# Rotary partners by transfers, square sums reordered ahead of one long sum, gated tiles split two steps later, in a two-block fp32 layer kernel

## The reference

```
x1, x2 = xr[..., :half], xr[..., half:]
rot = concatenate([x1 * c - x2 * s, x2 * c + x1 * s], axis=-1)
```

## Time and profile before

| what | value |
|---|---|
| median of 3 runs | 1926.7 us (1924.33 to 1930.63) |
| profiled execution, its time | 1925.77 us |
| profiled execution, its span | 1924.5 us |
| PE busy | 1909.5 us, 99% of the span |
| DVE, ACT, POOL busy | 1174.6, 880.2, 312.5 us |
| mean granted clock of PE | 0.996 |

### The profile page before, as it was taken

One profiled execution on the slowest core, in us unless ns is written; L12 is line 12 of the kernel. 1 busy time (PEld: TensorE's weight loads), 2 busy tenths in 40 slices (PEclk: granted clock), 3 DMA queues, 4 the chain that ended last, 5 costly groups with the idle time before them and its releaser, 6 DMA issues.

```text
span 1924.5 us, 37152 instructions
## 1 busy us (share of the span) xinstructions
PE 1909.5 (99%) x15818; PEld 1875.1 (97%) x15818; DVE 1174.6 (61%) x1709; ACT 880.2 (46%) x1265; POOL 312.5 (16%) x317
## 2 busy tenths in 40 slices
PE   9999999999999999999999999999999999999999
PEld 8999999999999999999999999999999999999987
DVE  6765666655555556645654765675467786555744
ACT  6444454544444434444444533445443333444443
POOL 3210010202110003300211252040011132110300
PEclk9999999999999999999999999999999999999999
DMA  7565545556666555565565563544564444566564
GB/s 259 155 198 180 162 155 156 176 186 188 196 189 195 196 192 183 185 202 195 191 237 196 167 217 121 154 132 130 156 183 146 133 143 138 181 199 195 194 232 154
DMA packets 175921, 343.80 MB, mean 179 GB/s; under 512 B 10495, under 2 KB 19579, under 8 KB 175227
## 3 DMA queue, kind: packets, MB, share of 16 engines
q1 hardware_dynamic: 174106, 337.16, 55.1%
q10 hardware_dynamic: 1648, 4.26, 0.6%
HBM read 335.09 MB, written 6.29 MB: 177 GB/s over the span
## 4 chain that ended last, share of the span: by engine, by line
PE 89%; issue 3%; DVE 2%; POOL 2%; ACT 0%; POOLq 0%; DVEq 0%; ACTq 0%
PE bank L1303 88%; DVE w_lo L1946 1%; POOL arena L2534 1%; DVE ob L2182 0%; POOL scratch L2540 0%; POOL arena L2543 0%; DVE hb L2182 0%; ACT w_hi L1638 0%; DVE scratch L2052 0%; POOL scratch L2551 0%; PE bank L1520 0%; PE bank L1610 0%; PE bank L1460 0%; PE bank L1458 0%; PE bank L1459 0%
## 5 line engine op out<-in xcount | busy, mean ns | idle before, releaser
L1946 DVE TENSOR_TENSOR w_lo<-w_raw,w_hi 128x1024 fp32r<-128x1024 f32 (+2 forms) x644 | 788.1, 1228 | 467.5 <-ACT w_hi L1638 465.4
L1638 ACT ACTIVATE w_hi<-w_raw 128x1024 fp32r<-128x1024 f32 (+2 forms) x644 | 662.4, 1032 | 874.2 <-PE bank L1303 863.9
L1303 PE MATMUL bank<-hb,w_hi 128*128 128x256 f32 x5284 | 957.1, 279 | 3.8 <-DVE w_lo L1946 2.1
L1303 PEld LDWEIGHTS bank<-hb,w_hi 128*128 128x128 f32 x5284 | 814.8, 188 | 7.4 <-DVE w_lo L1946 5.1
L1303 PE MATMUL bank<-ob,w_hi 128*128 128x256 f32 (+1 forms) x4060 | 773.4, 284 | 0.8 <-DVE w_lo L1946 0.8
L1303 PE MATMUL bank<-hb,w_lo 128*128 128x256 f32 x2448 | 678.1, 277 | 0.0
L1303 PEld LDWEIGHTS bank<-ob,w_hi 128*128 128x128 f32 x4060 | 635.4, 188 | 4.5 <-DVE w_lo L1946 1.2
L1303 PE MATMUL bank<-ob,w_lo 128*128 128x256 f32 (+1 forms) x2224 | 622.5, 280 | 0.0
L1303 PEld LDWEIGHTS bank<-hb,w_lo 128*128 128x128 f32 x2448 | 461.2, 188 | 0.0
L1303 PEld LDWEIGHTS bank<-ob,w_lo 128*128 128x128 f32 x2224 | 418.6, 188 | 0.0
L1303 PE MATMUL bank<-w_hi,ob 128*128 128x512 f32 (+1 forms) x384 | 104.2, 358 | 0.0
(11 more groups left out here) (239 smaller groups left out, 1039.9 us busy)
## 6 DMA issues: line engine op xcount, KB each, us to landing
w_raw<-in_w_in SPq DMA_DIRECT2D x436, 512.0 KB, 3.6
w_raw<-in_w_out SPq DMA_DIRECT2D x64, 512.0 KB, 4.3
w_raw<-in_w_o_conv SPq DMA_DIRECT2D x32, 512.0 KB, 4.1
w_raw<-in_w_o_mla SPq DMA_DIRECT2D x32, 512.0 KB, 4.0
w_raw<-in_w_branch SPq DMA_DIRECT2D x32, 512.0 KB, 3.7
w_raw<-in_w_kv_b SPq DMA_DIRECT2D x16, 512.0 KB, 3.9
w_raw<-in_w_q_b SPq DMA_DIRECT2D x16, 384.0 KB, 3.2
arena<-x_kept SPq DMA_DIRECT2D x2, 2048.0 KB, 9.8
```

Of the source, the lines that this page charges most:

```text
L1303: return nc.tensor.matmul(dst, lhsT, rhs, start=start, stop=stop, skip_group_check=True)
L1638: act(dst, src, ACT.Copy).then_inc(S_("w_hi"), 1)
L1946: tt(low, src, high.bitcast(F32), ALU.subtract).then_inc(S_("w_lo"), 1)
```

## The change

1. `rope` for the 28 tiles of `qr`, `qi`, `ka` and `qa` no longer uses PE. A new step `rope_swap` lets SP copy rows of x into the scratch buffer with partners exchanged (4 transfers for `qr` and `qi`, 2 for `ka` and `qa`; 128 rows of 1 KB in all), two pumps ahead of the step `rope`. The sign moves into the sine tables. DVE multiplies the scratch buffer by the sine table in place; POOL waits for the transfers before it writes x. The shared keys keep the products on PE (`rope_key`). A `qr` or `qi` job is two pumps longer, a `ka` or `qa` job one.
2. `row_sum` multiplies all but the last of the separate squares ahead of the accumulator.
3. After `row_sum` of `rp` come two of the constant products, then `row_spread`, then one (before: `row_spread`, then five).
4. The splits in `zconv`, `zmla`, `omla` and `bb` come 9 tiles after the evacuation, in `za` and `zb` still 7.

```diff
@@ _constants @@
-    put("rot_q1", rotation(RD, RD // 2, 1))
-    put("rot_a", rotation(P, 16, 1))
-    put("rot_i1", rotation(DI, 8, 1))
+        sign = np.where(o < half, -1.0, 1.0)[:, None]
+        return np.where(on, np.cos(ang), 1.0), np.where(on, sign * np.sin(ang), 0.0)
@@ plan_work @@
-    def rope(kind, k, ready, tables, rows=P):
-        dup = kind in ("kr", "ki")
-        b, s, b2 = side.take(), scratch.take(), None
...
+    def rope(kind, k, ready, tables):
+
+        sc = scratch.take()
+        landed = f"ld_rot{sc.slot}"
+        t = add("rope_swap", kind, k, dma=f"{landed} " * len(SWAPS[kind]), scratch=sc, ready=ready)
+        yield
+        yield
+        st = add("rope", kind, k, marks="rope_sin rope_out", scratch=sc, ready=ready, landed=t[landed], tables=tables)
+        sc.ends(st["rope_out"])
         done[kind, k] = st["rope_out"]
...
             def split_y():
                 done["oc", k] = add("conv_split", j, m, marks="op_hi op_lo", y=s["gated"])["op_lo"]
                 conv_free[m] = [("oc", k)]
-            later(split_y, 7)
+            later(split_y, 9)
...
-            later(split_y, 7)
+            later(split_y, 9 if name == "zm" else 7)
...
     post = row_factor("rp", [done["out_sq"]], extra=out_extra)
+    next(post)
+    warm(2)
     post_bank, done["rp"] = yield_of(post)
-    warm(5)
+    warm(1)
...
-        yield
-        yield
-        rope("ka", k, s["normed"], "late")
+        yield
+        yield from rope("ka", k, s["normed"], "late")
...
-        yield
-        rope("qa", h, s["qa_scaled"], "late")
+        yield from rope("qa", h, s["qa_scaled"], "late")
@@ new table @@
+SWAPS = {"qr": [(at + to, at + 32 - to, 32) for at in (0, 64) for to in (0, 32)],
+         "qi": [(at + to, at + of, n) for at in (0, 64) for to, of, n in ((0, 8, 8), (8, 0, 56))],
+         "qa": [(0, 16, 16), (16, 0, 112)]}
+SWAPS["ka"] = SWAPS["qa"]
@@ sync_engine @@
+    def rope_swap(s):
+        x, use = m.rope_of(*s.args)[0], s.of["scratch"]
+        sp.wait_ge(*use.after)
+        sp.wait_ge(*s.of["ready"])
+        for to, of, n in SWAPS[s.args[0]]:
+            dma(m.scratch[use.slot][to:to + n, 0:x.shape[1]], x[of:of + n, :]).then_inc(S_(f"ld_rot{use.slot}"), 16)
@@ tensor_engine, row_sum @@
+        early, late = s.of["extra"][:-1], s.of["extra"][-1:]
+        for i, (use, mark) in enumerate(early):
+            pe.wait_ge(*mark)
+            for j, lo in enumerate(starts):
+                mm(b[0:w, j:j + 1], m.scratch[use.slot][0:rows, lo:lo + w], ones[0:rows, 0:1], i == 0 and j == 0, False)
         for mark in s.of["squares"]:
             pe.wait_ge(*mark)
@@ vector_engine @@
     def rope(s):
+        x, _, cos, sin, _, _ = m.rope_of(*s.args)
+        partner = m.scratch[s.of["scratch"].slot][:, 0:x.shape[1]]
+        ve.wait_ge(*s.of["landed"])
+        ve.wait_ge(*done[s.of["tables"]])
+        tt(partner, partner, sin, ALU.mult).then_inc(S_("rope_sin"), 1)
@@ pool_engine, rope @@
+        po.wait_ge(*s.of["ready"])
+        po.wait_ge(*s.of["landed"])
```

More of the change, by code:

```diff
@@ L64, in rotation @@
             if o < half:
-                r[base + o + half, m] = -1.0
+                r[base + o + half, m] = 1.0
             elif o < 2 * half:
@@ L387, in factor, with rope_key @@
         done[what] = s["rf_out"]
-    def rope(kind, k, ready, tables, rows=P):
-        dup = kind in ("kr", "ki")
-        b, s, b2 = side.take(), scratch.take(), None
-        st = add("rope", kind, k, marks="rope_rot rope_sin rope_out" + (" rope_dup rope_cos" if dup else ""),
-                 bank=b, scratch=s, ready=ready, tables=tables, dup=Use(side, 0, NEVER))
+    def rope_key(kind, ready, tables):
+        b, s, b2 = side.take(), scratch.take(), side.take()
+        st = add("rope_key", kind, 0, marks="rope_rot rope_sin rope_out rope_dup rope_cos",
+                 bank=b, scratch=s, ready=ready, tables=tables, dup=b2)
         b.ends(st["rope_sin"])
+        b2.ends(st["rope_cos"])
         s.ends(st["rope_out"])
-        if dup:
-            b2 = st.of["dup"] = side.take()
-            b2.ends(st["rope_cos"])
+        done[kind, 0] = st["rope_out"]
+    def rope(kind, k, ready, tables):
[6 more added lines that the diff above has]
+        sc.ends(st["rope_out"])
         done[kind, k] = st["rope_out"]
@@ L402, in rope_later @@
         yield
-        rope(kind, k, ready, tables)
+        if kind == "kr":
+            rope_key(kind, ready, tables)
+        else:
+            yield from rope(kind, k, ready, tables)
         for _ in range(rest):
@@ L788, in ki_job @@
         yield
[L789 removed]
+        rope_key("ki", s["ki_gain"], "late")
         pending.extend(index_head(h) for h in range(HI))
@@ L1382, in row_sum @@
         for j, lo in enumerate(starts):
-            inst = mm(b[0:w, j:j + 1], squares[0:rows, lo:lo + w], ones[0:rows, 0:1], j == 0, not s.of["extra"])
-        for use, mark in s.of["extra"]:
+            inst = mm(b[0:w, j:j + 1], squares[0:rows, lo:lo + w], ones[0:rows, 0:1], j == 0 and not early, not late)
+        for use, mark in late:
             pe.wait_ge(*mark)
@@ L1434, in rope @@
         mm(m.side[b.slot][:, 0:w], rot[0:rows, :], x[0:rows, :]).then_inc(S_("rope_rot"), 1)
[L1435 to L1438, removed]
+        b = s.of["dup"]
+        pe.wait_ge(*b.after)
+        mm(m.side[b.slot][:, 0:w], dup[0:rows, :], x[0:rows, :]).then_inc(S_("rope_dup"), 1)
     def scores1(s):
@@ L2508, in rope @@
     def rope(s):
-        x, rot, cos, sin, dup, rows = m.rope_of(*s.args)
-        if dup is None:
-            po.wait_ge(*s.of["ready"])
-            po.wait_ge(*s["rope_rot"])
-            po.wait_ge(*done[s.of["tables"]])
-            t = po.step(tt(x, x, cos, ALU.mult))
-            po.wait_ge(*t)
-            po.wait_ge(*s["rope_sin"])
-            tt(x, x, m.scratch[s.of["scratch"].slot][:, 0:x.shape[1]], ALU.add).then_inc(S_("rope_out"), 1)
+        x, _, cos, _, _, _ = m.rope_of(*s.args)
+        po.wait_ge(*s.of["ready"])
+        po.wait_ge(*s.of["landed"])
+        po.wait_ge(*done[s.of["tables"]])
+        t = po.step(tt(x, x, cos, ALU.mult))
+        po.wait_ge(*t)
+        po.wait_ge(*s["rope_sin"])
+        tt(x, x, m.scratch[s.of["scratch"].slot][:, 0:x.shape[1]], ALU.add).then_inc(S_("rope_out"), 1)
     def clear_meta(s):
```

37 lines of the change are left out of this document (18 added, 19 removed).

## The result

The changed kernel takes 1909.5 us in the median of four runs (1907.83 to 1910.57), the kernel before 1925.5 us on the same chip (four runs, 1924.09 to 1930.63). The ratio is 0.992, 95% interval 0.9905 to 0.9934. The profiled execution took 1908.9 us. The forecast was 1910.0 us.

A forecast was written before the change was run, and what follows sets the result against it. PE was taken as the bound. Terms -12.2 + 0.5 - 0.5 - 3.5 - 1.0 = -16.7 us took the profiled 1925.8 to 1909.1, or 1910 us against the median of 1926.7; range 1905 to 1918.

The forecast's parts named there:

- Rotary products, -12.2 us: `q`, `qi`, `ka`, `qa`: 28 products leave PE, 24 at 0.43 us and 4 at 0.46, all of it gained.
- Waits for landings, +0.5 us: Rotary stages: DVE now waits for swap transfers to land; +0.5 us in all, bounds 0 and 7.
- a tie at 4.1 us: `q`: a swap lands 0.4 + 1.9 + 1.8 = 4.1 us on, DVE comes to it after some 4.2 us.
- rival C: `q`: DVE waits 1 to 2 us per landing, costing 7.6 us, so 1917 to 1918 us (1920 with later stages); chance 0.10.
- a sign of being wrong: `q` or `ka`: the prediction is wrong if PE waits for `w_lo` there; no size given.
- Rival D: Swaps in `q` and `qi`: four transfers land one after another, 7.2 us after issue; +31 us, so 1941; chance 0.06.
- Later splits, -3.5 us: `zconv` and `zmla`: five PE waits for `w_lo` go, 0.69 us each; bounds 3.5 and 0.
- End of wout, -1.0 us: End of `wout`: `qi` starts up to 2.3 us sooner, less a clock cost; -1.0, between -2.5 and +1.5.
- `qi` at the lower clock: Start of `qi`: after PE idles about 1 us, up to 5 us at half pace cost 2.5 us.
- Attention's jobs, -0.5 us: Moved job queue: a 1.6 us eviction stall goes, a new meeting can cost as much; -0.5, between -1.6 and +2.

The follow-up runs named there:

- no_swap: The kernel before with the later splits and the reordered end of `wout`, rotary products still on PE; 1920.4 us, ratio 0.9976.
- eight_issues: The changed kernel with each swap transfer cut in two by columns, 176 issues for the same bytes; 1944.5 us.
- split7: The changed kernel with every split of a gated or merged tile back at 7 tiles; 1914.7 us, 1914.1 without one run of 2081 us.
- early_q: The changed kernel with DVE's and POOL's rotary steps of `q` one pump later behind their swap, three instead of two; 1907.4 us.
- both: The changed kernel with every second swap transfer issued by ACT and the rotary steps of `q` one pump later; 1908.0 us, ratio 0.9897.
- pool_queue: The changed kernel with all 88 swap transfers issued by POOL instead of SP; 1931.8 us.

## Why the prediction was right

**Rotary products, -12.2 us: right.** In the aligned starts a swap's unit is 0.24 + 0.19 = 0.43 us shorter in `q` and in `qi`, as read from the earlier trace rows. The median of no_swap, which keeps these products, is 10.9 us higher; that is net of the waits for landings and holds some clock and pace (above). DVE's product itself took 0.42 us from SBUF as it had from PSUM.

**Waits for landings, +0.5 us: the term that was mis-sized.** It measured about 5 us: `q` gained 1.1 us where eight products are 3.44, and 1085 to 1172 us gained 0.7 where eight more are 3.44, so 2.3 + 2.7. The issue was taken as 0.47 us from the earlier trace rows, and it was 0.60 in `q` and 0.75 behind `qi`. For `q` I had written that the landing is a tie at 4.1 us after the first issue; it came to 4.25 (89.42 to DVE's start at 93.67) and 5.9 (93.56 to 99.42). In the second the issues took 2.4 us (1.9 forecast) and the time behind the last of them 3.45 (1.8 forecast), so in `q` the larger miss is behind the issues; what holds those transfers is open. For `qi` I had counted DVE's room and not SP's, which was full. So rival C happened in small: its place was right, and its price in `q` was 2.3 us and not 7.6, since DVE waited at six of the eight swaps and PE felt it at three places. One of the three is a wait of PE for `w_lo`, 0.5 us at 101.9 us. The prediction had named that as a sign of being wrong, and for this term it was.

**Rival D's mechanism** didn't occur at its size. The last of four transfers landed 1.4 us after its issue ended (1128.10 + 3.01 = 1131.11, DVE at 1132.53), and not after four landings of 1.8 us in a row. The Trainium skill's rule on disjoint parts ("DMA: Bandwidth & Descriptors", section "Rules for kernel authors") did not show as added time of that size, and the 1941 us of rival D did not come; with issues 0.6 to 0.75 us apart, a shorter transfer could still wait for its neighbour unseen. The other half of that rule, one transfer in place of several, is borne out, through the issues: eight_issues took 1944.5 us. The late landings of `q` stand behind weight loads (two were issued in the 1.7 us ahead of the swap at 93.56). That page's section "Queues, rings and completion order", by which each engine takes descriptors in ring order, would have it so, but no run here tests it.

**Later splits, -3.5 us: the stalls right, the sum 1.1 us more.** The table has -4.61, in all kernels with the delay alike. Five stalls of 0.61 to 0.76 us are the 3.5; most of the rest is a slow pace of PE behind the stall at 747.6 us (last section).

**End of wout, -1.0 us: right in sign, its parts not.** At its place it measured -2.9, a little over the start up to 2.3 us sooner. I had set against it `qi` at the lower clock, 2.5 us; this cost 1.3 to 1.6 and only in some kernels. That not all of it can be kept was right: 2.3 of the 2.8 us were given back from 1085 to 1172 us, through pace and a longer wait of PE there. What is left is 0.6 us in the profiles and 0.8 to 2.3 in the medians.

**Attention's jobs, -0.5 us.** The stall of 1.6 us at ACT's L1863 is gone and one of 1.5 at L1885 has come, so 0.1. But from 1172 to 1430 us the gain was 6.76 where twelve products are 5.3; the other 1.5 us is the pace of PE, which was slow before from 1381 us and is slow now only from 1418 us.

The misses are +4.6 for landings, -1.1 for splits, -1.9 for the end of `wout`, -1.0 for attention, -0.8 at the start (where the granted clock at 34 to 37 us was 1.00 and not the lower one) and -0.2 late. They add up to -0.4. The total was nearer than its parts: a miss of 4.6 us one way and of 5.0 the other cancelled, and that is luck. Some 2.7 us of the latter (0.8 at the start, 0.9 behind a stall, 1.0 in attention) are clock and pace, for which the sum had no term.

## What to carry to other kernels

For these transfers of 8 to 119 KB between partitions an issue held SP for 0.59 us in the median, 0.51 at least, and half the bytes cost the same (8 issues in 6.0 us): count issues, not bytes, and compare a full round of that queue (swap and weight load) with a unit of the bound engine, as is done for a compute engine. Where the queue has room, as in `q`, a longer lead helps as well. To start a transfer elsewhere, choose a program that waits for nothing the transfer leads to. An engine's stall can cost more than its length if what follows runs at another pace, so compare aligned instructions and not only idle times. And follow a gain to the end: time won at one place can be given back at the next one that another engine limits.

## What was not expected of the hardware

PE has two paces at one granted clock. Ordinary products of 256 columns follow each other every 113 ns in some stretches and every 118 ns in others (12 in 1.360 or 1.413 us), with both clocks at 1.00 and no idle time. Windows of the same length in the same stage, first of the changed kernel and then of split7:

```profile
1080.00:1120.00 40.00, 40.00 (x341) 40.00 (x340) 33.80 (x53) 22.35 (x35) 16.70 (x17) 1.00 0.75 241
```

```profile
1080.00:1120.00 40.00, 40.00 (x355) 40.00 (x354) 35.08 (x52) 24.54 (x41) 16.86 (x19) 1.00 0.75 239
```

PE is busy for 40.00 of 40.00 us in both and did 341 and 355 products; the starts show the same two steps. Many changes of pace stand at a stall or at products of another kind, but not all: in the kernel before it turned slow at the `w_lo` stall at 747.6 us, which adds 0.9 us to the price of that stall, and fast again at 771 us, where the trace shows neither. One long slow stretch, until about 1815 us in early_q, is the +4.8 to +5.0 of early_q, both and pool_queue in the table's last stretch. Over an execution the slow stretches add 1 to 10 us to what the fastest of these kernels show at the same products, as much as any single edit here, and they limit what a median of five runs can tell. What sets the pace was not tried.
